# The last layer's up projection in seven block products

## The reference, cut to what matters

```python
def _conv_ffn(h, w_up, conv_w, conv_b, w_down):
    u = _causal_dwconv(h @ w_up, conv_w, conv_b)   # h: 256 x 1024, w_up: 1024 x 5632, 3 taps
    a, b = jnp.split(u, 2, axis=-1)
    return (jax.nn.gelu(a) * b) @ w_down           # w_down: 2816 x 1024
...
        h = _rmsnorm(x, f_norm_g[l])
        x = x + _conv_ffn(h, f_w_up[l], f_conv_w[l], f_conv_b[l], f_w_down[l])
    return _rmsnorm(x, final_norm_g)
```

## Time and profile before

| | us |
|---|---|
| median of 3 runs | 1648.95 |
| lowest and highest | 1647.46, 1650.25 |
| the profiled execution's own time | 1647.94 |
| its span | 1646.1 |
| PE, PEld busy in the span | 1581.9, 1000.3 |
| DVE, ACT, POOL busy | 553.5, 238.3, 96.8 |
| the matmuls of up slabs 1 to 10 | 138.3 |

### The profile page before, as it was taken

The page is one execution under the profiler, slowest core; times in us unless marked ns, Lnnn a source line. Parts: engine busy times, 40 slices in busy tenths (PEclk is TensorE's granted clock), DMA queues, the critical chain, the costliest instruction groups (busy, mean ns, idle before and its releaser), DMA issues.

```text
span 1646.1 us, 22020 instructions
## 1 busy us (share of the span) xinstructions
PE 1581.9 (96%) x9033; PEld 1000.3 (61%) x9033; DVE 553.5 (34%) x1137; ACT 238.3 (14%) x528; POOL 96.8 (6%) x165
## 2 busy tenths in 40 slices
PE   8999899999998999999998889989999999999998
PEld 7754455555554687755544444447658867688853
DVE  4311011101111465213111111113987563445664
ACT  4110011001101232110100000004022212200000
POOL 2300000000000000029300000000000000000000
PEclk9999999999999999999999999999999999999999
DMA  9999999999999753899999999999423453444410
GB/s 329 421 407 409 425 424 427 426 424 425 425 427 411 266 204 129 361 404 421 426 428 426 426 425 427 428 423 366 151 85 146 146 212 103 144 153 151 150 56 25
DMA packets 104330, 512.75 MB, mean 311 GB/s; under 512 B 16986, under 2 KB 46011, under 8 KB 70331
## 3 DMA queue, kind: packets, MB, share of 16 engines
q1 hardware_dynamic: 102827, 507.55, 76.5%
q10 hardware_dynamic: 1424, 4.09, 0.7%
HBM read 506.38 MB, written 5.24 MB: 311 GB/s over the span
## 4 chain that ended last, share of the span: by engine, by line
PE 70%; DMA 24%; DVE 4%; SPq 1%; issue 0%; ACT 0%; DVEq 0%; ACTq 0%
DMA ring<-in_w_up 23%; PE PS L1069 18%; PE PS L1678 9%; PE PS L925 8%; PE PS L1118 7%; PE PS L1385 5%; PE PS L1103 4%; PE PS L1012 2%; PE PS L900 2%; PE PS L1596 2%; PE PS L1580 1%; PE PS L1396 1%; PE PS L1540 1%; PE PS L1090 1%; PE PS L882 1%; DVE arena L2594 1%
## 5 line engine op out<-in xcount | busy, mean ns | idle before, releaser
L1069 PE MATMUL PS<-ring,arena 128*64 128x256 f32 x3968 | 448.4, 382 | 40.1 <-DMA ring<-in_w_up 30.9
L1069 PEld LDWEIGHTS PS<-ring,arena 128*64 128x64 f32 x3968 | 287.4, 137 | 215.3 <-DMA ring<-in_w_up 44.7
L2410 DVE TENSOR_TENSOR arena<-PS,arena 128x256 f32<-128x256 f32 x64 | 27.2, 425 | 739.6 <-ACT arena L1836 739.6
L1118 PE MATMUL PS<-ring,arena 128*64 128x512 f32 x992 | 226.3, 598 | 2.7 <-DMA ring<-in_w_down 1.4
L1118 PEld LDWEIGHTS PS<-ring,arena 128*64 128x64 f32 x992 | 66.3, 136 | 153.1 <-issue 149.6
L1678 PE MATMUL PS<-hT,ring 128*128 128x256 f32 x640 | 138.3, 379 | 0.0
L1678 PEld LDWEIGHTS PS<-hT,ring 128*128 128x128 f32 x640 | 121.6, 190 | 16.5
L1103 PE MATMUL PS<-arena,hT 64*128 64x512 f32 x512 | 126.9, 615 | 0.0
L1844 ACT ACTIVATE arena<-PS 128x256 f32<-128x256 f32 x64 | 24.6, 385 | 496.4 <-PE PS L1090 496.4
L1385 PE MATMUL PS<-hT,ring 128*128 128x256 f32 x384 | 85.6, 384 | 0.0
L1853 ACT ACTIVATE arena<-PS 128x512 f32<-128x512 f32 x64 | 38.2, 597 | 299.6 <-PE PS L1118 299.6
(11 more groups left out here) (467 smaller groups left out, 1518.6 us busy)
## 6 DMA issues: line engine op xcount, KB each, us to landing
ring<-in_w_gate SPq DMA_DIRECT2D x62, 2048.0 KB, 23.8
ring<-in_w_up SPq DMA_DIRECT2D x62, 2048.0 KB, 25.6
ring<-in_w_down SPq DMA_DIRECT2D x62, 2048.0 KB, 24.6
ring<-in_f_w_up SPq DMA_DIRECT2D x22, 1024.0 KB, 6.6
ring<-in_w_in SPq DMA_DIRECT2D x9, 2048.0 KB, 19.3
ring<-in_f_w_down SPq DMA_DIRECT2D x5, 2048.0 KB, 7.5
arena<-in_w_gate SPq DMA_DIRECT2D x2, 2048.0 KB, 19.7
ring<-in_wo SPq DMA_DIRECT2D x2, 2048.0 KB, 10.5
```

The lines of the kernel that those rows point to most:

```text
L1069: mm = pe.matmul(PS[half * WINDOW:(half + 1) * WINDOW, bank, m * half_f:(m + 1) * half_f], xw[bank][:, k, :], mat(k, F_EXP)[:, half * half ...
L1118: mm = pe.matmul(PS[half * WINDOW:(half + 1) * WINDOW, 2 if own_room(e) else 3, :], hidT[:, 1 if own_room(e) else w, k * WINDOW:(k + 1) * ...
```

## The change

The up projection of slabs 1 to 10 gets seven block products too; slab 0 stays as it was. The transposed form is used: a block of weights (128 x 128) is stationary and 128 tokens move.

- **PE.** `up_product(j, v, h)` issues 4 matmuls (the pairs of the depth, `q`) with 128 tokens moving, for product v and half h of the columns: 7 x 2 x 4 = 56 matmuls for a slab in place of 32. Products 1, 2, 3 and 7 take blocks of the slab, products 5, 6 and 4 the sums. PE waits for the sums of weights (`pool_sums`) ahead of product 7, the fourth in order.
- **PSUM.** The seven partial results of a slab take four banks, 0-3 and 4-7 in turn. PE again starts slab j when slab j-2 has been read. The down projection's banks are 4, 5, 6, 7, 2, 3, 1, so it now waits for slab 9's reading at its start and for slab 10's ahead of product 5.
- **GpSimd.** `sum_parts` computes the sums of weights of up slabs 1 to 10 and of down slabs 0 and 1, four instructions of 128 x 1024 each, as `weight_sums` does. The sums for slab n are released when slab n-2 is done, those of slabs 1 and 2 when the cross attention before is done. VectorE keeps down slabs 2 to 5.
- **VectorE.** `row_sums("up")`, four instructions of 128 x 512, once, after the activations are scaled. For each slab `gated` of the slab before now comes first, then `add_up_partials`: a copy and seven additions of 128 x 256 that build the four output blocks in SBUF (`rows4`, the other `cacc`), then `conv`, which now reads SBUF. The one-element copy after `conv` (L2846) is gone.

```diff
@@ -584,6 +585,28 @@
...
+        def up_sums(j):
+            return up_sum[0] if j == 1 else up_sum[1 + j % 2]
...
+        def up_partial(j, v):
+            at = 4 * (j % 2) + (v - 1) // 2, (v - 1) % 2 * T
+            return PS[:, at[0], at[1]:at[1] + T]
...
@@ -1659,42 +1682,81 @@
...
+            def up_product(j, v, h):
+
+                b, sums = up_slab(j), up_sums(j)
+                for q in range(KD // 2):
+                    one = slice(q, q + 1)
+                    rows = lambda token, odd: pair_rows("up", one, token, odd)[:, 0, :]
+                    added = lambda i: sum_rows("up", i, one)[:, 0, :]
+                    if v == 1:
+                        x, w = rows(0, 0), b[:, q, 0, h, 0, :]
+                    if v == 2:
+                        x, w = rows(0, 1), b[:, q, 1, h, 0, :]
+                    if v == 3:
+                        x, w = added(2), b[:, q, 1, h, 1, :]
+                    if v == 4:
+                        x, w = rows(1, 1), sums[2][:, q, h, :]
+                    if v == 5:
+                        x, w = added(0), sums[0][:, q, h, :]
+                    if v == 6:
+                        x, w = added(1), sums[1][:, q, h, :]
+                    if v == 7:
+                        x, w = rows(1, 0), b[:, q, 0, h, 1, :]
+                    mm = pe.matmul(up_partial(j, v)[:, h * P:(h + 1) * P], w, x, start=(q == 0), stop=(q == KD // 2 - 1))
+                return mm
+
...
                 turn_halves(7 * TT)
                 for j in range(FFN_UP):
                     n = FFN_UP0 + j
                     slab_wait(n)
                     w = slab(n).rearrange("p (k h n) -> p k h n", k=KD, h=2)
-                    if j >= 2:
+                    if j == 0:
...
+                        mm.then_inc(s["slabs_done"], 1)
+                        continue
+                    if j == 1:
+                        scaled_step(2, 0)
+                        scaled_step(2, KD // 2)
+                    else:
                         pe.wait_ge(s["ffn_read"], j - 1)
-                    x = hT if j else h_ffn
-                    for h in range(2):
-                        for f in range(2):
-                            for k in range(KD):
-                                if j == 0 and h == 0 and f == 0:
-                                    hT_step("ffn", k)
-                                if j == 1 and h == 0 and f == 0:
-                                    scaled_step(2, k)
-                                mm = pe.matmul(PS[:, 2 * (j % 2) + h, f * T:(f + 1) * T], w[:, k, h, f * P:(f + 1) * P], x[:, k, :], start=(k == 0), stop=(k == KD - 1))
-                            if j == 0 and h == 0 and f == 0:
-                                spread_roots("ffn")
+                    for v in (1, 2, 3, 7, 5, 6, 4):
+                        if v == 3:
+                            pe.wait_ge(s["row_sums"], ROW_SUMS["up"] + 1)
+                        if v == 7:
+                            pe.wait_ge(s["pool_sums"], j)
+                        for h in range(2):
+                            mm = up_product(j, v, h)
                     mm.then_inc(s["slabs_done"], 1)
                 last = FFN_PAIRS - 1
                 for j in range(FFN_DOWN - 2):
...
-                    pe.wait_ge(s["weight_sums"], WEIGHT_SUMS["ffn"] + j + 1)
+                    if j < 2:
+                        pe.wait_ge(s["pool_sums"], FFN_UP - 1 + j + 1)
+                    else:
+                        pe.wait_ge(s["weight_sums"], WEIGHT_SUMS["ffn"] + j - 1)
+                    if j == 0:
+                        pe.wait_ge(s["ffn_read"], FFN_UP - 1)
                     for v in range(1, 8):
-                        if j == 0 and v >= 5:
-                            pe.wait_ge(s["ffn_read"], FFN_UP - (v < 7))
+                        if j == 0 and v == 5:
+                            pe.wait_ge(s["ffn_read"], FFN_UP)
                         mm = seven_product("ffn", v, down_pairs(j), last)
...
@@ -2829,35 +2891,49 @@
...
+                def add_up_partials(j, c):
+
+                    part = lambda v: up_partial(j, v).rearrange("p (h n) -> p h n", h=2)
+                    block = lambda token, half: c[:, half:half + 3:2, token * P:(token + 1) * P]
+                    step(dve.tensor_copy(block(0, 0), part(1)))
+                    step(dve.tensor_tensor(block(0, 1), block(0, 0), part(6), ALU.add))
+                    dve.tensor_tensor(block(0, 0), block(0, 0), part(2), ALU.add)
+                    step(dve.tensor_tensor(block(1, 0), block(0, 1), part(7), ALU.add))
+                    dve.tensor_tensor(block(1, 1), block(1, 0), part(5), ALU.add)
+                    step(dve.tensor_tensor(block(0, 1), block(0, 1), part(5), ALU.add))
+                    dve.tensor_tensor(block(1, 0), block(1, 0), part(4), ALU.subtract)
+                    dve.tensor_tensor(block(0, 1), block(0, 1), part(3), ALU.add).then_inc(s["ffn_read"], 1)
+                    dve.wait_ge(s["ffn_read"], j + 1)
+
+                for h in range(2):
+                    dve.wait_ge(s["h_scaled"], 2 + h + 1)
+                row_sums("up", slice(0, KD // 2))
                 for j in range(FFN_UP):
                     dve.wait_ge(s["slabs_done"], FFN_UP0 + j + 1)
-                    if j >= 2:
-                        dve.wait_ge(s["ffn_g"], j - 1)
...
+                    rows4 = cacc[(j + 1) % 2]
                     if j == 0:
...
-                        step(last)
-                    conv(cacc[j % 2], lambda f: PS[:, 2 * (j % 2) + f // 2, f % 2 * T:(f % 2 + 1) * T] if j else scaled[:, f, :], taps,
-                         [vec("f_conv_b_2", c) for c in chunks]).then_inc(s["ffn_read"], 1)
-                    dve.wait_ge(s["ffn_read"], j + 1)
-                    dve.tensor_copy(dummy, ident[0:1, 0:1]).then_inc(s["ffn_conv"], 1)
+                        last.then_inc(s["ffn_read"], 1)
+                        dve.wait_ge(s["ffn_read"], 1)
+                    else:
+                        gated(j - 1)
+                        add_up_partials(j, rows4)
+                    conv(cacc[j % 2], lambda f: rows4[:, f, :], taps, bias).then_inc(s["ffn_conv"], 1)
                     if j:
-                        gated(j - 1)
                         row_sums("ffn", slice(j - 1, j))
-                    if j in (FFN_UP - 3, FFN_UP - 2):
-                        weight_sums("ffn", j - (FFN_UP - 3))
                 gated(FFN_UP - 1)
                 row_sums("ffn", slice(FFN_UP - 1, FFN_UP))
...
@@ -2991,12 +3067,35 @@
...
+            def sum_parts(parts, sums):
+
+                b11, b12, b21, b22 = parts
+                step(pool.tensor_tensor(sums[0], b12, b11, ALU.subtract))
+                pool.tensor_tensor(b12, b22, b12, ALU.subtract)
+                step(pool.tensor_tensor(sums[1], b22, sums[0], ALU.subtract))
+                pool.tensor_tensor(sums[2], sums[1], b21, ALU.subtract).then_inc(s["pool_sums"], 1)
+
+            def ffn():
+                for j in range(1, FFN_UP):
+                    n = FFN_UP0 + j
+                    pool.wait_ge(loaded(n), slab_bytes_due(n))
+                    pool.wait_ge(s["slabs_done"], FFN_UP0 if j < 3 else n - 1)
+                    if j == 3:
+                        pool.wait_ge(s["ffn_read"], 1)
+                    sum_parts(up_parts(j), up_sums(j))
+                for j in range(2):
+                    n = FFN_DOWN0 + j
+                    pool.wait_ge(loaded(n), slab_bytes_due(n))
+                    pool.wait_ge(s["slabs_done"], n - 1)
+                    sum_parts(pair_parts("ffn", j), weight_sum["ffn"][j])
+
```

More of the change, by code:

```diff
@@ L586, in pair_slab, with up_slab, up_parts, pair_parts @@
             return slab(first_pair_slab[stage] + j)[:, 0:2 * D * pairs].rearrange("p (q h n) -> p q h n", h=2, n=D)
+        up_sum = [tuple(v.rearrange("p (q h n) -> p q h n", q=KD // 2, h=2) for v in vs) for vs in (
+            [ar(at, 1024) for at in (9088, 10496, 14856)],
+            [ar(16000 + 1024 * i, 1024) for i in range(3)],
+            [ar(12928 + 1024 * i, 1024) for i in range(3)])]
+        def up_sums(j):
+            return up_sum[0] if j == 1 else up_sum[1 + j % 2]
+        def up_slab(j):
+            return slab(FFN_UP0 + j).rearrange("p (q o h f n) -> p q o h f n", q=KD // 2, o=2, h=2, f=2)
+        def up_parts(j):
+            return [up_slab(j)[:, :, odd, :, half, :] for odd in range(2) for half in range(2)]
+        def pair_parts(stage, j, pairs=2):
+            v = pair_slab(stage, j, pairs)
+            return [v[:, :, odd, half * 512:(half + 1) * 512] for odd in range(2) for half in range(2)]
+        def up_partial(j, v):
+            at = 4 * (j % 2) + (v - 1) // 2, (v - 1) % 2 * T
+            return PS[:, at[0], at[1]:at[1] + T]
         def sum_rows(stage, i, ks):
```

28 lines of the change are left out of this document (19 added, 9 removed).

## The result

The changed kernel takes 1678.5 us in the median of four runs (1678.4 to 1680.7), the kernel before 1648.9 (1647.5 to 1650.3): a ratio of 1.0186, 95% interval 1.0173 to 1.0198. The profiled execution has a span of 1676.7 us and an own time of 1678.45.

The account below looks back on a forecast made before the run. PE was taken to bound the kernel before, VectorE in turns with GpSimd after. Terms of +2, -2.6, +14 and +12.3 sum to 25.7 us, added to the median 1648.95: 1675 us, range 1657 to 1686.

Parts of the forecast that it names:

- Passes of 111.7 ns, slabs of 12.5 us: PE in up slabs: 128-column passes take 111.7 ns, a slab 12.5 us; ten save 13 us if nothing waits.
- VectorE's own 10.0 us: VectorE's work for one up slab, without waits for GpSimd, totals 10.0 us, under PE's 12.5.
- Turns at 128x1024: VectorE and GpSimd alternate whole instructions on SBUF; GpSimd's of 128x1024 take about 2.3 us each.
- The start: Slab 1: six VectorE instructions each wait for one of GpSimd's; it ends at 1451 against 1449, +2 us.
- A steady slab of 15.8 us: Slabs 4 to 10: VectorE, taking turns with GpSimd, sets a period of 15.8 us against 13.8, +14 us.
- Down slab 0: First down slab waits for VectorE's reading of slab 10, ending 19.1 us after PE's last up slab: +12.3 us.
- The turns cost little: Rival: GpSimd might yield within a long instruction; PE binds again, all 13 us come, 1636 us; chance 0.14.
- A longer lag: Rival: GpSimd instructions of 2.45 us or more also catch `gated`, up to 3.5 us more a slab; chance 0.08.

Follow-up runs that it names:

- e1: Changed kernel with GpSimd's four weight-sum subtractions a slab replaced by one small write; 1635.7 us, ratio 0.9924 to the kernel before.
- e6: Changed kernel with slabs' output blocks in PSUM (slab 0's convolution still reads SBUF) and GpSimd's first sums waiting for `row_sums("up")`; 1655.5 us.
- e13: Changed kernel with 12 further multiplications (24 passes of 128 columns) ahead of PE's wait for PSUM in slabs 4 to 10; 1676.6 us.

## The prediction against the runs

1675 us was forecast, 1678.5 came, inside the range of 1657 to 1686. Span by span, from the two traces (the forecast terms sum to 25.7 us, the measured ones to 30.6, the difference of the two spans):

| stretch (us) | before | after | forecast | measured |
|---|---|---|---|---|
| to the stage's start | 1419.07 | 1418.03 | 0 | -1.0 |
| to the end of slab 1 | 30.1 | 32.4 | +2 | +2.4 |
| slabs 2 and 3 | 27.6 | 25.0 | -2.6 | -2.6 |
| slabs 4 to 10 | 96.7 | 114.6 | +14 | +17.9 |
| from there to the end | 72.7 | 86.6 | +12.3 | +13.9 |

- **Passes of 111.7 ns, slabs of 12.5 us.** Right, and e1 shows that all 13 us come if nothing waits.
- **VectorE's own 10.0 us.** Right: 9.8 in e1. The additions from PSUM keep 0.41 to 0.42 under GpSimd.
- **Turns at 128x1024.** Right, the step I trusted least: e6's 2.29 and 2.23 us, and in the changed kernel 412 or 478 ns in the median with a maximum of 2.53 and 2.58. The TENSOR_SCALARs do contend.
- **The start.** +2 was right in size and half right in place. The token sums held PE 1.1 us. I missed that the roots' own TENSOR_SCALARs (L2885) are caught too: 2.20 us each where 0.28 is their time, and PE waited 2.0.
- **A steady slab of 15.8 us.** The mean is 16.4, with the wait of 2.7 us ahead of slab 4, but there is no steady state: from start to start it is 16.1, 16.7, 15.5, 24.0, 14.6, 12.5, 12.5. The step assumed one set of sums in each program of VectorE. GpSimd is released by PE, and where VectorE is late, two sets fall into one program. That one slab of 24.0 and two of 12.5 bring the mean so near is in part luck. The turns themselves were priced about right: in e13, where further passes fill PE's waits and make its own slab 15.5 us, the slabs do settle, and VectorE, which does not wait for PE there either, takes 15.5 and 16.0 us in turn.
- **Down slab 0.** VectorE's last reading ended 18.7 us behind the last up slab, forecast 19.1. PE waited 2.9 + 5.7 us. The slow clock took 3.0 us more in the first 12 passes (8.31 for 5.32), but these lie ahead of the second wait, whose end VectorE sets, and only shortened it. The 2.0 us that it took in the 8 passes behind that wait (5.60 for 3.60) came on top: 18.7 + 5.2 + 2.0 - 12.0 = 13.9. The clock was in no term of mine, and these 2.0 us are what it was short of here.
- **The rivals.** "The turns cost little" fell in every run with sums beside SBUF operands. "A longer lag" came once, ahead of slab 8: `gated` was caught, by 2.1 us, because two sets fell together.
